# Gate rows and window sums as high and low rounded products, and the high weights of a slot first

## What is computed

```python
def modulation(cond, w, b, n):
    m = jax.nn.silu(cond) @ w[:, :n * D_MODEL] + b[:n * D_MODEL]
    return jnp.split(m, n, axis=-1)

def odd_mixer(h, w_pool, pool_scale, w_out, grid):
    xp, gate = jnp.split(h, 2, axis=-1)
    ...
    z = jnp.stack([centred_window_mean(g, w, 1) - g for g, w in zip(groups, POOL_WINDOWS)], axis=-2)
    z = jnp.einsum('brcgi,gio->brcgo', z, w_pool).reshape(bn, L, POOL_W) * pool_scale
    return (z * jax.nn.silu(gate)) @ w_out

# second_block, for each of the two layers
sh, sc, gt = modulation(c_lat, w_ada[i], b_ada[i], 3)
u = x * (1.0 + sc) + sh
y = even_mixer(u @ w_in_e, ...) if i % 2 == 0 else odd_mixer(u @ w_in_o, ...)
x = layer_norm(alpha * x + gt * y, ln_g[i], ln_b[i])
```

## Time and profile before

| | |
|---|---|
| median of 3 runs | 1716.3 us (1714.3 to 1716.99) |
| profiled execution | 1715.85 us, of which the span is 1714.1 us |
| PE busy | 98% of the span, 8036 matmul instructions |
| DVE, ACT, POOL busy | 77%, 52%, 9% |
| DMA | 390.59 MB, 228 GB/s in the mean |
| granted clock of PE over the span | 0.99 |

### The profile page before, as it was taken

The page is one execution under the profiler, slowest core; times in us unless marked ns, Lnnn a source line. Parts: engine busy times, 40 slices in busy tenths (PEclk is TensorE's granted clock), DMA queues, the critical chain, the costliest instruction groups (busy, mean ns, idle before and its releaser), DMA issues.

```text
span 1714.1 us, 22141 instructions
## 1 busy us (share of the span) xinstructions
PE 1678.5 (98%) x8036; PEld 1389.9 (81%) x8036; DVE 1327.3 (77%) x1731; ACT 894.2 (52%) x1341; POOL 155.2 (9%) x222
## 2 busy tenths in 40 slices
PE   9999999999999999999999989999999999999996
PEld 8888888888888888878877878888777778878885
DVE  6978778879877878587975777778876978667766
ACT  6447564445466654565843466666534374444432
POOL 1100000001100000011211110000101101110000
PEclk9999999999999999999999999999999999999998
DMA  8955554658755545689987953444959869886653
GB/s 322 328 194 194 179 168 160 209 176 296 271 172 173 185 146 192 224 283 352 356 264 228 309 177 125 133 134 157 316 182 344 314 230 316 280 263 226 227 198 111
DMA packets 111410, 390.59 MB, mean 228 GB/s; under 512 B 16253, under 2 KB 17165, under 8 KB 109805
## 3 DMA queue, kind: packets, MB, share of 16 engines
q1 hardware_dynamic: 74944, 268.99, 44.8%
q0 software_dynamic: 27856, 101.19, 19.0%
q10 hardware_dynamic: 8510, 19.08, 3.1%
HBM read 385.02 MB, written 4.19 MB: 227 GB/s over the span
## 4 chain that ended last, share of the span: by engine, by line
PE 90%; DVE 5%; ACT 2%; DMA 2%; issue 1%; ACTq 0%; DVEq 0%; SPq 0%
PE L L370 25%; PE L L372 24%; PE L L371 24%; PE TP L475 3%; PE AB L2399 2%; DMA stage<-in_w_stream 1%; PE AB L2097 1%; PE AB L2005 1%; DVE wl L323 1%; PE TP L2110 1%; PE AB L2415 1%; PE AB L2332 1%; PE AB L2100 1%; PE AB L2123 1%; PE AB L2122 1%
## 5 line engine op out<-in xcount | busy, mean ns | idle before, releaser
L370 PE MATMUL L<-wh,xth 128*128 128x512 f32 (+1 forms) x1948 | 788.8, 405 | 7.8 <-DVE wl L323 5.1
L302 ACT ACTIVATE wh<-stage 128x1024 fp32r<-128x1024 f32 x504 | 530.5, 1057 | 509.3 <-PE L L372 386.0
L323 DVE TENSOR_TENSOR wl<-stage,wh 128x1024 fp32r<-128x1024 f32 x504 | 612.5, 1220 | 236.0 <-ACT wh L302 235.1
L372 PE MATMUL L<-wh,xtl 128*128 128x512 f32 (+1 forms) x1948 | 762.8, 392 | 0.0
L371 PE MATMUL L<-wl,xth 128*128 128x512 f32 (+1 forms) x1948 | 761.6, 391 | 0.0
L370 PEld LDWEIGHTS L<-wh,xth 128*128 128x128 f32 x1948 | 368.6, 189 | 85.0 <-DVE wl L323 9.2
L372 PEld LDWEIGHTS L<-wh,xtl 128*128 128x128 f32 x1948 | 367.8, 189 | 77.9
L371 PEld LDWEIGHTS L<-wl,xth 128*128 128x128 f32 x1948 | 368.8, 189 | 74.4 <-issue 4.1
L648 DVE SCALAR_TENSOR_TENSOR macc<-mstage,scols,macc 128x1024 f32<-128x1024 f32 x240 | 306.7, 1278 | 5.4 <-DMA mstage<-in_w_mod 4.8
L699 POOL DMA_DIRECT2D mstage<-in_w_mod x192 | 138.9, 724 | 1269.0 <-DVE macc L648 1004.2
L769 ACT ACTIVATE pa<-pa,st 128x128 f32<-128x128 f32 x96 | 43.0, 450 | 68.2 <-DVE st L1325 37.6
(11 more groups left out here) (237 smaller groups left out, 1316.2 us busy)
## 6 DMA issues: line engine op xcount, KB each, us to landing
stage<-in_w_stream SPq DMA_DIRECT2D x504, 512.0 KB, 4.5
mstage<-in_w_mod POOLq DMA_DIRECT2D x192, 512.0 KB, 6.2
arena<-in_ctx ACTq DMA_DIRECT2D x1, 2048.0 KB, 9.8
x_kept<-X ACTq DMA_DIRECT2D x4, 512.0 KB, 8.9
X<-x_kept ACTq DMA_DIRECT2D x1, 2048.0 KB, 9.7
arena<-in_b_ada ACTq DMA_DIRECT2D x2, 1024.0 KB, 10.2
arena<-in_ln_g ACTq DMA_DIRECT2D x2, 1024.0 KB, 9.9
X<-in_x SPq DMA_DIRECT2D x3, 512.0 KB, 8.4
```

Source lines behind the costliest of these rows:

```text
L302: nc.scalar.activation(wh[:, s % SPLITS].rearrange("p a b -> p (a b)"), stage[:, s % RING, :], ACT.Copy).then_inc(hi_ready, 1)
L323: nc.vector.tensor_tensor(wl[:, s % SPLITS].rearrange("p a b -> p (a b)"), stage[:, s % RING, :], wh[:, s % SPLITS].rearrange("p a b -> p ...
L370: nc.tensor.matmul(o, xh, w[0], start=start, stop=False, skip_group_check=True)
L372: last = nc.tensor.matmul(o, xl, w[0], start=False, stop=True, skip_group_check=True)
```

## The change

Three edits. (1) A slot's 12 products are reordered. First come the eight with the high weights (xth·wh and xtl·wh, by half and token tile), behind a wait for `hi_ready`; then the four with the low weights, behind a wait for `lo_ready`. (2) A gate row is made from two rounded parts of `macc`: ACT copies a high part (`gate_row_high`), DVE subtracts it for a low part (`gate_row_low`), and PE multiplies both by a rounded matrix of ones. (3) The window sums do the same with Z (`z_high` on ACT, `z_low` on DVE) and with windows that ACT has copied into the rounded format once. The parts lie in buffers that are there already: `tailr`, and the flat views of `lxh` (flat[0]) and `lxl` (flat[1]).

```diff
@@ slot products
+        def high_products(dst, slot, kt, start, x=(xth, xtl), tiles=range(TT), width=COLS):
+            for k in range(KPB):
+                for t in tiles:
+                    w = wh[:, slot, k, 0:width]
+                    xh, xl = (v[:, kt + k, t * P:t * P + P] for v in x)
+                    nc.tensor.matmul(dst[:, t, 0:width], xh, w, start=start and k == 0, stop=False, skip_group_check=True)
+                    nc.tensor.matmul(dst[:, t, 0:width], xl, w, start=False, stop=False, skip_group_check=True)
+        def low_products(dst, slot, kt, x=(xth, xtl), tiles=range(TT), width=COLS):
+            for k in range(KPB):
+                for t in tiles:
+                    last = nc.tensor.matmul(dst[:, t, 0:width], x[0][:, kt + k, t * P:t * P + P], wl[:, slot, k, 0:width],
+                                            start=False, stop=True, skip_group_check=True)
+            return last
         def slot(pe, n, G, kt, start, x=(xth, xtl), width=COLS):
             if start:
                 pe.wait_ge(psum_free, G + 1)
+            pe.wait_ge(hi_ready, n + 1)
+            high_products(L[G % 2], n % SPLITS, kt, start, x, width=width)
             pe.wait_ge(lo_ready, n + 1)
-            for k in range(KPB):
-                last = products(L[G % 2], n % SPLITS, k, kt + k, start and k == 0, x, width=width)
-            last.then_inc(split_free, 1)
+            low_products(L[G % 2], n % SPLITS, kt, x, width=width).then_inc(split_free, 1)
...
@@ ACT
+            def gate_row_high(layer, half):
+                act.wait_ge(mod_sum, mod_done(0, (11 if layer else 8) + half))
+                if layer and not half:
+                    act.wait_ge(once("pool_sums"), 4)
+                high, _, acc = gate_sums(layer, half)
+                nc.scalar.activation(high, acc, ACT.Copy).then_inc(once("gate_row_hi"), 1)
             nc.scalar.activation(ar(0, 2048), ar(0, 2048), ACT.Silu).then_inc(once("gate_silu"), 1)
+            gate_row_high(0, 0)
             split_pairs(act, split_hi, R_G + BESIDE, 1, evac_to(6144, 0, 1024))
...
+                if n == 7:
+                    gate_row_high(0, 1)
...
+                if n in (30, 38, 46, 54):
+                    g = (n - 30) // 8
+                    if g:
+                        act.wait_ge(once("pool_sums"), g)
+                    nc.scalar.activation(z_high, Z[:, :, COLS * g:COLS * g + COLS], ACT.Copy).then_inc(once("z_high"), 1)
+                if n == 59:
+                    gate_row_high(1, 0)
...
@@ DVE
+            def gate_row_low(layer, half):
+                high, low, acc = gate_sums(layer, half)
+                dve.wait_ge(once("gate_row_hi"), 2 * layer + half + 1)
+                if half:
+                    dve.wait_ge(once("gt_ready"), 4 * layer + 2)
+                elif layer:
+                    dve.wait_ge(once("pool_sums"), 4)
+                nc.vector.tensor_tensor(low, acc, high.bitcast(F32), ALU.subtract).then_inc(once("gate_row_lo"), 1)
...
+                if n in (31, 39, 47, 55):
+                    g = (n - 31) // 8
+                    dve.wait_ge(once("z_high"), g + 1)
+                    if g:
+                        dve.wait_ge(once("pool_sums"), g)
+                    nc.vector.tensor_tensor(z_low, Z[:, :, COLS * g:COLS * g + COLS], z_high.bitcast(F32), ALU.subtract)\
+                        .then_inc(once("z_low"), 1)
...
@@ PE, modulation_gate
-                pe.wait_ge(mod_sum, mod_done(0, (11 if layer else 8) + half))
-                    nc.tensor.matmul(AB[c % 2][:, :], ones[:], macc[:, (c // 2 + 1 - layer) % 2, COLS * (c % 2):COLS * (c % 2) + COLS],
-                                     start=True, stop=True).then_inc(once("gt_ready"), 1)
+                pe.wait_ge(once("gate_row_lo"), 2 * layer + half + 1)
+                    nc.tensor.matmul(AB[c][:, :], ones_r[:], high[:, cs], start=True, stop=False)
+                    nc.tensor.matmul(AB[c][:, :], ones_r[:], low[:, cs], start=False, stop=True).then_inc(once("gt_ready"), 1)
@@ PE, pool_sums
+                pe.wait_ge(once("z_low"), g + 1)
-                        last = nc.tensor.matmul(AB[t][:, :], WIN[:, min(g, 2), j, P * t:P * t + P],
-                                                Z[:, j, COLS * g:COLS * g + COLS], start=j == 0, stop=j == tiles[-1])
+                        nc.tensor.matmul(AB[t][:, :], w, z_high[:, j, :], start=j == 0, stop=False)
+                        last = nc.tensor.matmul(AB[t][:, :], w, z_low[:, j, :], start=False, stop=j == tiles[-1])
```

More of the change, by code:

```diff
@@ L274, in decays, with gate_sums @@
             return sums_of[hd % 2][:, a:a + 1024]
+        def gate_sums(layer, half):
+            high = flat[0][:, 0:1024] if half else tailr[:].rearrange("p a b -> p (a b)")
+            return high, flat[1][:, 0:1024], macc[:, (half + 1 - layer) % 2, :]
+        z_high, z_low = tailr[:], flat[1][:, 0:1024].rearrange("p (t n) -> p t n", t=TT)
+        windows_r = flat[0][:, 0:1024], flat[0][:, 1024:1280]
         def halves(v, b):
@@ L397, in last_slots @@
                     if t == 0:
+                        pe.wait_ge(hi_ready, n + i + 1)
+                    high_products(L[G % 2], (n + i) % SPLITS, kt + KPB * i, False, tiles=[t])
+                    if t == 0:
                         pe.wait_ge(lo_ready, n + i + 1)
-                    for k in range(KPB):
-                        last = products(L[G % 2], (n + i) % SPLITS, k, kt + KPB * i + k, False, tiles=[t])
+                    last = low_products(L[G % 2], (n + i) % SPLITS, kt + KPB * i, tiles=[t])
                     if t == 1:
@@ L1879, in _ @@
                     turn_plain(n + 1)
+                if n == 8:
+                    gate_row_low(0, 1)
                 if n == 9:
@@ L2238, in modulation_gate @@
             def modulation_gate(layer, half):
-                pe.wait_ge(mod_sum, mod_done(0, (11 if layer else 8) + half))
-                for c in (2 * half, 2 * half + 1):
+                high, low, _ = gate_sums(layer, half)
+                pe.wait_ge(once("gate_row_lo"), 2 * layer + half + 1)
+                for c in range(2):
                     if half:
-                        pe.wait_ge(once("gt_done"), 4 * layer + c - 1)
-                    nc.tensor.matmul(AB[c % 2][:, :], ones[:], macc[:, (c // 2 + 1 - layer) % 2, COLS * (c % 2):COLS * (c % 2) + COLS],
-                                     start=True, stop=True).then_inc(once("gt_ready"), 1)
+                        pe.wait_ge(once("gt_done"), 4 * layer + c + 1)
+                    cs = slice(COLS * c, COLS * c + COLS)
+                    nc.tensor.matmul(AB[c][:, :], ones_r[:], high[:, cs], start=True, stop=False)
+                    nc.tensor.matmul(AB[c][:, :], ones_r[:], low[:, cs], start=False, stop=True).then_inc(once("gt_ready"), 1)
             def low_rank(n):
@@ L2505, in slot_tile @@
                     pe.wait_ge(psum_free, G + 1)
+                turned(pe, uses[QUADS.index((s // 2, t))])
+                pe.wait_ge(hi_ready, 8 * R_ODD0 + s + 1)
+                high_products(L[G % 2], s % SPLITS, KPB * s, s == 0, tiles=[t])
                 pe.wait_ge(lo_ready, 8 * R_ODD0 + s + 1)
-                turned(pe, uses[QUADS.index((s // 2, t))])
-                for k in range(KPB):
-                    last = products(L[G % 2], s % SPLITS, k, KPB * s + k, s == 0 and k == 0, tiles=[t])
+                last = low_products(L[G % 2], s % SPLITS, KPB * s, tiles=[t])
                 if t:
```

24 lines of the change are left out of this document (19 added, 5 removed).

## The result

The change took 1706.05 us in the median of five runs (1704.87 to 1707.19), the kernel before in the same series 1716.99 (1714.3 to 1717.35). The ratio is 0.994 with an interval of 0.9926 to 0.9955: 10.3 us, or 7.7 to 12.7. The profiled execution took 1705.38 us with a span of 1703.5, against 1715.85 and 1714.1. The forecast was 1705.2.

What follows compares the result with a forecast made beforehand. PE, busy 98% of a 1714.1 us span, bounds the kernel; 7.6 (rounded format) + 3.5 (high weights first) = 11.1 us off 1715.85 gives 1704.75, with 0.45 a median of 1705.2; 8-in-10 range 1702 to 1711.5.

Steps and rivals of the forecast that it cites:

- Rounded format: Window sums and gate rows: 38 instructions go from 0.428 to 0.227 us, saving 7.6 us (4.4 and 3.2).
- High weights first: Slots where PE stalled: waiting for the low part only after eight high products saves 3.5 us, between 0 and 7.4.
- The four early stalls: Waits for DVE alone at 266, 622, 762 and 765: below 1.82 us, go whole, 2.2 us.
- At 1205: Slot waiting for ACT's copy behind a Silu, then DVE: gains 0.3 of 1.8 us, gate row 0's copy coming between.
- the stalls at 1324 and 1332: Slots before gate row 1, which comes 1.9 us earlier, 0.8 already counted under rounding, so 1.1 us.
- Satisfied waits: About 500 added waits, nearly all for something long done: cost nothing; at 0.11 us each it would be 55 us.
- Work added: Extra ACT copies and DVE subtractions for gate rows and window sums: hidden, cost 0, at most 1.2 + 1.0 us.
- Rival 1: Only the rounded format pays; PE waits in mid-slot for what it waited for at the start: 1708.7 us; chance 0.16.
- Rival 2: New ACT and DVE work comes late; all eight subtractions on the path return 9.8 us: 1715.0 us; chance 0.06.
- Rival 3: New order of products runs slower; 1.8 ns on each of 6,036 takes back the gain: 1716 us; chance 0.07.
- Rival 4: Eight bank changes per slot instead of four let PE's clock fall; 85 products at the low level make 1722; chance 0.05.
- the prediction's sign of a dip in a new place: PE's granted clock: the prediction called itself wrong if it dips in new places; no size given.

Runs made afterwards that it cites:

- turn_first: silu_later, with DVE making xtl of the turned tokens ahead of the modulation step in the convolution stage; 1703.08 us, ratio 0.9923.
- high_first_only: The kernel before with the new product order and two waits, gate rows and window sums still in fp32; 1711.89 us, ratio 0.9968.
- round_only: The change with the old product order and one wait, for the low part, at the slot's start; 1712.32 us, ratio 0.9976.
- low_wait_first: The change, new product order kept, with the wait for the low part moved to the slot's start; 1711.09 us, ratio 0.997.
- last_low_late: The change with the last window group's low part made behind the split of block 57 instead of 55; one run, 1713.26 us.
- after_again: The change itself, unaltered, run again on the chip of the first experiments; 1706.08 us, ratio 0.9945 to the kernel before.
- half_mod_loads: The change with half of the modulation weights not loaded in two stretches, so the output is wrong; 1702.55 us, ratio 0.9909.
- silu_later: The change with the gate's Silu behind ACT's fourth block copy and gate row 0's high part behind the fifth; 1704.83 us, ratio 0.9933.

## Why the prediction was right

**Rounded format, 7.6 us: 7.0.** Seven of the eight places give what the rows said: 1.17 for six instructions, 1.57 for eight and .81 or .82 for each four (worked out: 1.21, 1.61, .80). The eighth is gate row 0, where 0.20 came instead of 0.8, since PE then ran into a wait for `xtl` (0.42 idle at 1276.92, and the slow restart). That is the term that was too large. In turn_first, with `xtl` made earlier, it gives 0.44. The window sums' 4.36 for 22 instructions is 7.5 for 38, nearer to the 7.6 of the rows than to the 8.1, an estimate, that the prediction worked out from the Trainium skill ("FP8 and Floating Point Precision", section "TensorE Precision Notes").

**High weights first, 3.5 us: 4.3 in seven slots.** The four early stalls gave 2.34 for 2.2. At 1205 it was 0.10 for 0.3. The earlier trace rows has eight waits and the prediction listed seven; the eighth (0.20 idle at 1397.89) is gone too, under the new low stretch at slot 400. For gate row 0 and the stalls at 1324 and 1332 together I had 1.9, since DVE's residual sets the time there, and it was 0.20 + 1.87 = 2.07: what gate row 0 didn't give, these stalls did (high_first_only, with gate row 0 in fp32, has 2.16 at them). So the sum of the two terms is 11.3 for 11.1, and the two differences from the prediction, -0.6 and +0.8, mostly belong together.

**Satisfied waits, 0.** Right: a slot's first product behind a satisfied wait starts 0.22 us after the last matmul (1544.07), and a window sum's first behind three starts as close (1543.15).

**Work added, 0.** Right for the copies and subtractions of the change, and only because its parts cover each other. Not right for the kernel's end, where 0.7 us comes with the rounded parts. ACT's high part of gate row 0 took 0.2 more of the stall at 1205 than I worked out, and 0.8 to 1.0 us when the wait for the low part stood at the slot's start (round_only, low_wait_first). Cover at the last window sum was 0.8 for 0.7, and last_low_late shows what stands behind it.

**What the prediction did not have.** First, transfers give back. PE, ahead of its old time by 7 us at slot 235, meets blocks that land late. 2.4 us went back at slots 235 and 396 in the change, 3.1 in after_again, 3.9 in high_first_only, and 1.3 to 4.8 over the six traces that have the later wait and all loads. The lead alone doesn't set it: low_wait_first, with none, lost 0.57 at 235, and half_mod_loads, 6.2 us ahead, lost nothing. Second, the 0.7 us at the end. Third, the clock's places, 1.4 gained and 0.9 lost. With these the change is left with 11.3 - 2.4 - 0.7 + 1.4 - 0.9 = 8.7 us, inside the measured interval of 7.7 to 12.7, against a ratio that says 10.3 and a forecast of 11.1. The other 1.8 of the profiled pair's 10.5 are steps that differ from one execution to the next. So that the forecast came this close is partly luck: the give-back was missing from it, and how large it is in a mean execution isn't settled.

**The rivals.** Rival 1 (only rounding pays, 1708.7) is out: high_first_only alone has 0.9968. Its mechanism, a wait in mid-slot, is real at two places (1.3 us). Its number was wrong too: 1716.3 less round_only's 4.1 is 1712.2. Rival 2 (late ACT and DVE work) cost at most 0.2 at slot 340. Rival 3 (slower pace) is out by low_wait_first. Rival 4 (the clock) is out as a slower kernel, by the dense stretch (window of the change: PE busy, PEclk, DMA share, GB/s), against the earlier trace rows:

```profile
1400.00:1540.00 140.00, 140.00 (x625) 1.00 0.87 290
```

PE changes its accumulator bank 8 times in a slot there and the granted clock is 1.00; the total at the low level is 23.9 us before and after. But the prediction's sign of a dip in a new place did come, near 1387, in the same view:

```profile
1384.00:1392.00 8.00, 5.35 (x23) 0.79 0.35 122
```

PE there waits for turned tokens, and before has the same wait with the granted clock at 1.00 behind it (timeline of PE, the change, then before, and the window of before):

```profile
1387.57 0.77 PE L390 MATMUL L<-wh,xth 128*128 128x512 f32 x1 [2.65 <-issue]
```

```profile
1393.81 0.47 PE L370 MATMUL L<-wh,xth 128*128 128x512 f32 x1 [2.69 <-DVE xtl L1873]
```

```profile
1390.00:1398.00 8.00, 5.10 (x31) 1.00 0.36 123
```

The wait at 1376 isn't the cause, since half_mod_loads doesn't have it and has the dip (its window, the same columns):

```profile
1382.00:1389.00 7.00, 5.04 (x18) 0.76 0.21 75
```

Nor is it the order of products: low_wait_first has the new order and no dip here. All seven traces with the later wait have it, and the three without don't; why isn't shown. It costs 0.94 us at slot 400, and the shorter low stretch near 693 gives back more than that. The Trainium skill ("TensorE: Matmul & The Clock Gate", section "A second HAM failure mode: psum-queue depth-cycling") puts the swings of its kernel down to PE standing briefly between groups of matmuls as it cycles through banks. In the dense stretch the banks change and PE doesn't stand, and the clock doesn't move, so bank changes alone don't lower it here; the other half of the Trainium skill's account this stretch can't test. The other dip in a new place (high_first_only at 808, 0.83 in the window 804 to 814, and silu_later at 806.9) came behind a wait of 2.1 us.

## What to carry to other kernels

Follow the gain slot by slot, not in the total: each part of a change has its step there, and so has what is given back. When the engine that bounds a kernel gets faster, ask at which places its feeders' transfers already run late, and how many of its buffers cover them; the largest part of the price of a faster PE here was paid there. Compare the end of the kernel too, behind the last slot: here it took back 0.7 us that no slot shows. A wait is best placed at the first instruction that needs its data, since a satisfied one showed no cost here, and it then also covers other late work, as ACT's copy at 1205.

## What the runs showed of the hardware

- The 128x512 matmul in the rounded format starts every 0.227 us whatever the order of its operands and banks: xth·wh, xtl·wh and wl·xth, and also with a window or a row of sums as operand. In fp32 it stands as two instructions 0.428 us apart.
- A satisfied semaphore wait in front of a matmul costs nothing that the starts show (0.22 to 0.23). After a wait that did stop PE the second start comes 0.11 us later than usual, with 0.5 instead of 0.39 for the first matmul's length (1201.41 to 1201.74, 0.33). The same gap stands behind a run of transposes without a wait (before, 1288.21 to 1288.53).
- The granted clock's total at the low level was between 20.5 and 30.7 us in the ten traces (20 to 1690 us). Low stretches stood behind one-column matmuls or waits. The same wait of 2.7 us near 1390 was followed by one in the seven traces with the later wait and by none in the three without, low_wait_first with the new order of products among them; the wait of 1.32 us at 804.19 in the change was followed by none.
- The output's last transfer of 256 KB landed 3.6 us after its issue in the eight traces in which an 8 KB transfer of instructions ran beside it, and 2.9 us in the two in which none did.
